# Two buffers for the fill weights of attention and mLSTM, and the mLSTM chunks overlapped in program order, in a hybrid decoder block on one Trainium2 core

## The reference, cut to what matters

```python
# mLSTM: 4 heads of 64, chunks of 128 tokens (8 chunks), carry (C, n, m) from chunk to chunk
D = F[..., :, None] - F[..., None, :] + ig[..., None, :]          # causal
m_t = jnp.maximum(F + m0[..., None], jnp.max(D, axis=-1))
Sw = jnp.einsum('bhctd,bhcsd->bhcts', qc, kc) * jnp.exp(D - m_t[..., None])
num = einsum(Sw, vc) + inter[..., None] * einsum(C0, qc)
h = num / jnp.maximum(jnp.abs(den), jnp.exp(-m_t))[..., None]
h = h * lax.rsqrt(jnp.mean(h * h, axis=-1, keepdims=True) + EPS) * hn_g * jax.nn.sigmoid(o)
# sliding-window attention: 8 query heads, 2 key heads, blocks of 128, window 128, sinks
s = jnp.einsum('bnqkgd,bnskd->bkgnqs', qh, kb);  p = jnp.exp(s - m)
out = jnp.einsum('bkgnqs,bnskd->bnqkgd', p / den, vb)
# merge: g_a * (y_a @ w_br_a) + g_b * (y_b @ w_br_b) + g_c * (y_c @ w_br_c), g = sigmoid(h @ w_gate)
```

## Time and profile before

| | |
|---|---|
| median of 3 runs | 2003.87 us (2002.91 to 2469.56) |
| profiled execution, its own time | 1997.14 us |
| its span, first to last instruction | 1995.4 us |
| granted TensorE clock, mean | 0.960 of full speed |
| PE busy | 1839.7 us, 92% of the span |

### The profile page before, as it was taken

How to read it: one execution, slowest core, us unless ns; L and a number is a source line. 1 busy time by engine, 2 the same in 40 slices (tenths; PEclk the granted TensorE clock), 3 DMA queues, 4 the chain that set the end, 5 groups by cost and what they waited for, 6 DMA issues and landing times.

```text
span 1995.4 us, 37944 instructions
## 1 busy us (share of the span) xinstructions
PE 1839.7 (92%) x16145; PEld 1028.8 (52%) x16145; DVE 665.5 (33%) x1569; ACT 437.6 (22%) x999; POOL 230.5 (12%) x352
## 2 busy tenths in 40 slices
PE   6999999998998599999999999996999999999990
PEld 3454455554443255555555554554566565665550
DVE  4385344443343532333223333552211111000114
ACT  4220412221223321122121212111222222221210
POOL 3030000000000102221022214001000000000003
PEclk9999999998899799999999999996999999999995
DMA  9386010001112000101010028231999999999988
GB/s 312 110 281 220 11 32 21 21 21 32 42 42 65 17 24 24 30 14 30 17 30 22 21 108 307 108 127 65 388 393 395 392 393 393 390 388 388 388 319 319
DMA packets 146919, 334.03 MB, mean 167 GB/s; under 512 B 19274, under 2 KB 63224, under 8 KB 146844
## 3 DMA queue, kind: packets, MB, share of 16 engines
q1 hardware_dynamic: 127776, 282.68, 39.1%
q0 software_dynamic: 8240, 25.04, 3.8%
q10 hardware_dynamic: 10828, 25.24, 3.2%
HBM read 299.50 MB, written 37.63 MB: 169 GB/s over the span
## 4 chain that ended last, share of the span: by engine, by line
PE 84%; DMA 7%; DVE 3%; ACT 2%; issue 1%; POOL 1%; SPq 1%; ACTq 0%; POOLq 0%; DVEq 0%
PE bank L280 80%; DMA arena<-in_w_e_in 3%; DMA arena<-in_w_in 3%; PE bank L1189 1%; POOL arena L711 1%; PE bank L878 1%; DMA arena<-y_slots,ints 1%; PE bank L1206 1%; PE bank L1128 0%; PE bank L1208 0%; SPq L452 0%; DMA y_slots<-arena 0%; DVE arena L1748 0%; DVE arena L1826 0%; PE bank L754 0%
## 5 line engine op out<-in xcount | busy, mean ns | idle before, releaser
L280 PE MATMUL bank<-arena 128*32 128x256 f32 (+8 forms) x15294 | 1746.8, 380 | 60.2 <-DMA arena<-in_w_in 12.9
L280 PEld LDWEIGHTS bank<-arena 128*32 128x32 f32 (+4 forms) x15294 | 937.8, 134 | 811.3 <-issue 545.6
L2191 DVE TENSOR_TENSOR arena<-arena,bank 128x128 f32<-128x128 f32 x96 | 21.8, 283 | 369.8 <-ACT arena L1591 369.8
L1578 ACT ACTIVATE arena<-bank,arena 128x96 f32<-128x96 f32 x256 | 85.9, 441 | 11.8 <-PE bank L1189 11.8
L675 POOL DMA_INDIRECT arena<-xnorm,ints x32 | 31.6, 987 | 470.9 <-PE bank L1189 450.7
L2200 DVE TENSOR_TENSOR arena<-bank,arena 128x512 f32<-128x512 f32 x64 | 35.7, 558 | 134.6 <-PE bank L280 134.6
L1984 DVE TENSOR_TENSOR arena<-arena,bank 128x256 f32<-128x256 f32 x40 | 16.8, 421 | 172.8 <-PE bank L280 172.8
L626 POOL TENSOR_TENSOR arena<-arena 64x256 f32<-64x256 f32 x96 | 71.1, 741 | 28.7 <-DVE arena L1970 22.0
L1584 ACT ACTIVATE arena<-bank 128x384 f32<-128x384 f32 x32 | 15.7, 490 | 267.7 <-PE bank L1208 267.7
L1529 ACT ACTIVATE arena<-bank 128x256 f32<-128x256 f32 (+1 forms) x48 | 18.4, 382 | 208.7 <-PE bank L280 208.7
L1591 ACT ACTIVATE arena<-bank 128x128 f32<-128x128 f32 x96 | 19.7, 278 | 164.7 <-PE bank L280 164.7
(11 more groups left out here) (330 smaller groups left out, 1025.5 us busy)
## 6 DMA issues: line engine op xcount, KB each, us to landing
arena<-in_w_e_in SPq DMA_DIRECT2D x64, 2048.0 KB, 21.3
arena<-in_w_e_out SPq DMA_DIRECT2D x32, 2048.0 KB, 21.4
arena<-in_w_ada SPq DMA_DIRECT2D x12, 2048.0 KB, 12.4
arena<-in_w_in SPq DMA_DIRECT2D x32, 512.0 KB, 4.0
y_slots<-arena ACTq DMA_DIRECT2D x32, 288.0 KB, 6.3
y_slots<-arena POOLq DMA_DIRECT2D x21, 384.0 KB, 17.9
arena<-in_x SPq DMA_DIRECT2D x4, 1024.0 KB, 8.4
arena<-in_w_in SPq DMA_DIRECT2D x2, 2048.0 KB, 25.4
```

Of the source, the lines that this page charges most:

```text
L280: return nc.tensor.matmul(o, l, r, start=start, stop=stop)
L1578: ins = A.activation(e_xT[s][:, k, :], PS[k // 4][:, ts(k % 4, CAP)], ACT.Identity, scale=sc2[:, k:k + 1], bias=sh2[:, k:k + 1])
L2191: ins = TT(e_h[:, r, :], e_g[:, r, :], E_GU[r][:, P:2 * P], ALU.mult)
```

## The change

- SP loads the fill weights alternately into two views, `FWS[0]` and `FWS[1]`, with a semaphore each; the load for chunk f is issued when the fill of chunk f-2 is done. Attention and mLSTM form one sequence of 16 loads.
- Attention's score matmuls alternate between the partition halves (the loop over a is the inner one).
- mLSTM on PE: the opening of chunk c+1 (`b_mu`, scores, transposes of the keys: `front`) comes right after chunk c's fill, and the transposes of chunk c's y (`mlstm_turned`) come after fill 0 to 2 of chunk c+1. The first opening comes right after attention's last fill, and the last y of attention is transposed after the first three fill matmuls of mLSTM, in `PS[7]`. The products with the state come after fill 4 instead of fill 2.
- The mLSTM's temporaries move to places that are free earlier. POOL's copies for mLSTM chunk 0 come ahead of its copies for attention chunk 0; ACT copies the keys of chunk 0 ahead of attention and those of chunk c+1 in the middle of chunk c; DVE makes `b_wv` and `b_bd` of chunk 0 ahead of attention (`weighted`), those of chunk c+1 between L1887 and L1888 of chunk c.
- PE's attention loop and the mLSTM loops of all engines are written out in Python.

```diff
 # SP
-            with sp.Fori(1, NT) as c:
-                sp.wait_ge(sem("fill"), 2 * c)
-                columns(FW, 0, c)
...
+            def fill_columns(f):
+                sp.dma_start(FWS[f % 2], w_in[:, :, ds((0, OFF_G)[f // NT] + P * (f % NT), P)]).then_inc(s_fill[f % 2], 16)
...
+            fill_columns(0)
+            fill_columns(1)
...
+            for f in range(2, 2 * NT):
+                sp.wait_ge(sem("fill"), 2 * (f - 1))
+                fill_columns(f)
+                if f >= NT + 2:
+                    first_gate(f - NT - 1)
 # POOL
+            pool.wait_ge(sem("gates_dve"), B_CLEARED)
+            pool.wait_ge(sem("b_silu"), 4)
+            pool.wait_ge(sem("proj_out"), 34)
+            staged(0)
             def attn(c, first=False):
...
+            for c in range(NT):
                 pool.wait_ge(sem("b_exp"), c + 1)
                 G.tensor_tensor(b_e, b_e, U.unsqueeze(1).to_broadcast([P, H, P]), ALU.mult).then_inc(sem("b_masked"), 1)
+                if c < NT - 1:
+                    staged(c + 1)
 # PE
             def attn(c, first=False):
-                pe.wait_ge(sem("mix_staged"), c + 1)
-                for a in range(2):
-                    for i in range(4):
+                pe.wait_ge(sem("mix_staged"), c + 2)
+                for i in range(4):
+                    for a in range(2):
...
+            def front(c):
+                if c == 0:
+                    pe.wait_ge(sem("gates_act"), G_DONE)
+                    pe.wait_ge(sem("mix_done"), NT - 1)
+                    pe.wait_ge(sem("pa_out"), 2 * NT)
+                else:
+                    pe.wait_ge(sem("mix_staged"), NT + c + 1)
                 pe.wait_ge(sem("b_k"), c + 1)
                 pe.wait_ge(sem("b_bd"), c + 1)
                 mm(PS[0], ones[0:32, :], b_bd[0:32]).then_inc(sem("b_mu"), 1)
...
+            def mlstm(c):
+                fill(c, 0, 3)
+                if c:
+                    mlstm_turned(c - 1)
+                else:
+                    attn_turned(NT - 1)
+                fill(c, 3, 5)
+
+                if c:
                     pe.wait_ge(sem("b_state"), c)
                 pe.wait_ge(sem("b_kt"), c + 1)
                 pe.wait_ge(sem("b_arg"), c + 1)
+                pe.wait_ge(sem("b_wv"), c + 1)
+                pe.wait_ge(sem("mix_done"), NT + c)
...
+            for c in range(NT):
+                attn(c, c == 0)
+                if c < NT - 1:
+                    attn_turned(c)
+            front(0)
+            for c in range(NT):
                 mlstm(c)
+                if c < NT - 1:
+                    front(c + 1)
+            mlstm_turned(NT - 1)
 # ACT, mLSTM
+            for c in range(NT):
+                act.wait_ge(sem("b_scores"), c + 1)
...
                 A.activation(b_e, b_e, ACT.Exp, scale=-1.0).then_inc(sem("b_exp"), 1)
+                if c:
+                    mlstm_out(c - 1)
+                else:
+                    attn_out(NT - 1, PS[7])
...
                 A.activation(ga_o[:, 0:512], PS[5], ACT.Copy).then_inc(sem("ga_out"), 1)
+                if c < NT - 1:
+                    keys(c + 1)
                 root(b_ms, c + 1)
 # DVE, mLSTM
+            def weighted(c):
+                dve.wait_ge(sem("mix_staged"), NT + c + 1 if c else 1)
+                TT(b_wv, b_v, bc(g_w[:, ts(c, 4)], 65), ALU.mult).then_inc(sem("b_wv"), 1)
...
                 lk(TT(b_h, b_h, PS[4][:, 0:260].rearrange("p (h n) -> p h n", h=H), ALU.add))
+                if c < NT - 1:
+                    weighted(c + 1)
                 lk(STT(b_d, b_h[:, :, 64], -1.0, b_h[:, :, 64], ALU.mult, ALU.max))
```

More of the change, by code:

```diff
@@ L925, in mlstm, with mlstm_turned @@
                 ins.then_inc(sem("b_scores"), 1)
-                fill(c, first, 0, 3)
-                if not first:
+            def mlstm_turned(c):
+                pe.wait_ge(sem("mix_y"), NT + c + 1)
+                for p in range(2):
+                    ins = E.transpose(PS[7][:, ts(2 + p, P)], b_hh[:, 2 * p:2 * p + 2, :].rearrange("p a n -> p (a n)"), ident)
+                ins.then_inc(sem("mix_yT"), 1)
+            def mlstm(c):
[6 more added lines that the diff above has]
+                if c:
                     pe.wait_ge(sem("b_state"), c)
@@ L939, in mlstm @@
                 ins.then_inc(sem("b_inter"), 1)
-                fill(c, first, 3, 8)
+                fill(c, 5, 8)
                 pe.wait_ge(sem("b_sw"), c + 1)
@@ L944, in mlstm @@
                 ins.then_inc(sem("b_num"), 1)
[L945 to L951, removed]
+                fill(c, 8, 16)
+            for c in range(NT):
[4 more added lines that the diff above has]
+            for c in range(NT):
                 mlstm(c)
+                if c < NT - 1:
+                    front(c + 1)
+            mlstm_turned(NT - 1)
             pe.wait_ge(sem("mix_done"), NT + NT)
@@ L1438, in attn, with attn_out, keys @@
                 A.activation(c_pT[:, 4:8, :], PS[3], ACT.Copy).then_inc(sem("c_pT_out_a"), 1)
+                if not last:
+                    attn_out(c, PS[0])
+            def attn_out(c, bank):
                 act.wait_ge(sem("mix_yT"), c + 1)
-                A.activation(QC[:, :, ts(c, P)], PS[0].rearrange("p (i n) -> p i n", i=4), ACT.Copy).then_inc(sem("mix_done"), 1)
-            with act.Fori(0, NT) as c:
+                A.activation(QC[:, :, ts(c, P)], bank.rearrange("p (i n) -> p i n", i=4), ACT.Copy).then_inc(sem("mix_done"), 1)
+            def keys(c):
+                if c:
+                    act.wait_ge(sem("b_scores"), c)
+                A.activation(b_k, QK[:, 2:4, ts(c, P)], ACT.Copy, scale=N ** -0.5).then_inc(sem("b_k"), 1)
+            act.wait_ge(sem("b_silu"), 4)
+            keys(0)
+            with act.Fori(0, NT - 1) as c:
                 attn(c)
+            attn(NT - 1, True)
             def root(v, n):
@@ L1898, in mlstm @@
                 TT(b_hh, b_hh, VO[:, ds(c, 1), 256:512].rearrange("p o (h n) -> p (o h) n", h=H), ALU.mult).then_inc(sem("mix_y"), 1)
-            with dve.Fori(0, NT) as c:
+            for c in range(NT):
                 mlstm(c)
-            chain[0] += 11 * NT
             dve.wait_ge(sem("mix_done"), NT + NT)
```

127 lines of the change are left out of this document (52 added, 75 removed).

## The result

The changed kernel takes 1949.46 us (median of 4 runs, 1948.21 to 1950.37), the kernel before on the same chip 2003.39 (4 runs). The ratio is 0.9757, with a 95% interval of 0.9737 to 0.9778: 2.4% faster. It is taken from the fast runs alone, while the median of 2003.39 still counts one slow run of 2469.56, so the quotient of the two medians differs from it. The profiled execution took 1950.37 us, its span is 1948.6 us against 1995.4, so 46.8 us have to be found.

What follows compares the result with a forecast made beforehand. PE's waits and slow clock were taken as the bound. Savings of 11.1 (attention), 5.0 (transition) and 27.9 (mLSTM), 44.0 us, took 1997.14 to 1953.1; adding 6.7 for the median gave 1959.9 us, range 1950 to 1976.

Steps and rivals of the forecast that it cites:

- The median: Whole kernel: the median of runs lies 6.7 us above the profiled execution, raising 1953.1 to 1959.9 us.
- Attention, seams: Attention between chunks: load wait gone and scores alternating, seam 1.93 instead of 3.65 us, 12.0 us saved over 7 seams.
- The rival that the order does nothing: Attention's scores: alternating the halves gains nothing, 7.7 us lost, total 1967.6 us; chance 0.08.
- What is late next: Attention's exponentials and mLSTM's copy of y still come in time for PE, with margins of 0.4 and about 1 us.
- rival 2: Attention's exponentials or mLSTM's copy of y become new waits, 1 us in 15 chunks, total 1974.9 us; chance 0.14.
- The beginning: Attention's start: PE waits for four POOL copies, partly repaid by the new score order; cost 0.8 to 0.9 us.
- Transition: Attention to mLSTM: the first opening waits only for DVE's L1841, not for freed temporaries; 5.0 us saved.
- mLSTM: mLSTM stage: both seam waits and the clock stretch go, eight chunks at 18.43 us, 147.6 against 175.50, 27.9 us saved.
- rival 1: PE's clock still dips at mLSTM seams and attention's start because of weak work, total 1975.1 us; chance 0.17.
- rival 4: Written-out bodies, 16 on PE, must be fetched and stall; at 5.3 us a body 2% slower, 2044 us; chance 0.04.

Runs made afterwards that it cites:

- e_order: The kernel before with only attention's score matmuls alternating between the partition halves: 2006.31 us, ratio 1.0049.
- e_buffers_order: The kernel before with both two fill-weight views and attention's alternating scores: 1972.21 us, ratio 0.9866.
- e_turn_first: The changed kernel with each mLSTM chunk's y transposed at its old place, ahead of the next chunk's opening: 1949.17 us, ratio 0.9765.
- e_copies_first: The changed kernel with POOL's copies for attention chunk 0 again ahead of those for mLSTM chunk 0: 1949.36 us, ratio 0.9746.
- e_buffers: The kernel before with only the two fill-weight views, PE's and SP's chunk loops written out: 1979.20 us, ratio 0.9917.
- the two last ones: e_copies_first, 1949.36 us, and that kernel with attention's fill halves in two banks, y turned in PS[7] and DVE's token shift later, 1940.22 us.
- e_keys_late: The changed kernel with ACT's copy of the next chunk's keys at the end of the chunk, not its middle: 1961.96 us, ratio 0.9836.

## Why the prediction was right, and where its terms were off

The sign, the size and its split over three stages were right. 1949.46 lies half a microsecond below the range's lower end at 1950, and the sum was 44.0 against 46.8 us.

**The median.** Only 2.8 of the 10.4 us between forecast and result lie in the sum. The forecast added 6.7 us, by which the first median (2003.87) stood above the profiled run. The changed kernel's median is 0.9 below its profiled run, which makes the other 7.6. The kernel before's medians beside the later runs, 1994.9 to 1997.1, show that 2003.87, the middle of three runs, was a high one. From 1997 the same sum would have given 1953.

**Attention, seams.** 7 seams at 1.72 were forecast, 12.0 us; a chunk takes 22.67 us as forecast and the stage is 12.5 shorter. By the traces, counted from the first score to the next fill, the seven seams gave 12.6, since the waits for the load differ (0.65 to 1.04). The lower clock at the start took 1.5 back, the new order of chunk 0 gave 1.0, and 0.4 is the last turn of y, which moved. But the two parts of a seam are no separate terms. The order alone brought 1.4 us (e_order), the views alone 5.7, and both 13.4 (e_buffers_order). The sum had the right total because the change makes both. The rival that the order does nothing fell: the scores take 2.00 us, as in the earlier trace rows. Where the prediction weighed the Trainium skill, "TensorE: Matmul & The Clock Gate", Part 3 (matmuls in strict program order), the old order was to take about 3.3 us by the rule (the prediction's estimate). The kernels here with the old order show 2.96 and those with the new one 2.00, and the sum rightly went by the row.

**What is late next.** The margins held. In the changed kernel the exponentials' last step ends 0.4 us before PE's transposes start (348.92 and 349.36), and ACT's copy of y 1.1 before the state products, 0.4 and 1 by the forecast. (The sum in the text, 373.16 + 3.30 + 0.19, is 376.65 and not 376.5. The last two steps overlap by 0.1 us, so the margin stands.) Neither attention's exponentials nor mLSTM's copy of y is among PE's waits (rival 2).

**The beginning.** PE was forecast to wait for four copies, and waits 2.51 us instead of 0.78. The cost in the sum was 0.9. It was more like 1.7 + 1.5 less 0.96, 2.3 us, because the clock fell to 0.50 there in this execution. e_turn_first, the same up to mLSTM but without that dip, shows 1.7 less 0.96, as forecast. e_copies_first took both away, and the total did not follow.

**Transition.** 5.0 forecast, 4.4 to 4.9 measured, depending on whether attention's last turn of y, which moved behind the boundary, is counted.

**mLSTM.** 27.9 forecast, 30.3 measured. The idle term was right (15.2 against 15.1). The rest is a mis-sized term: a chunk takes 18.09 and not 18.43 us, 2.7 us in eight. The 18.43 was the busy time of a chunk with two idle times in it, and the ends of matmuls are modelled. A last record ahead of an idle time is counted whole, though its tail would lie under the next one. "No idle, full clock" is best read from a stretch that has neither.

**The clock, rival 1.** The result was as forecast, full clock, but the argument against the rival was not sound. It rested on chunk 5, whose seam kept a full clock with 2.36 us of idle time. e_order has the same mLSTM instructions, 2.6 us earlier, and all its seams dip, with 24.3 us of stretch. That the timing decides is the reading left by the two traces; it was not tried by itself. The start of attention bears it out: the same instructions after the same 2.5 us of idle time ran at 0.50 in the changed kernel and at 1.00 in e_turn_first. So the full clock was forecast rightly, but not for a reason that held. What the runs support is only that in all four kernels without idle time in mLSTM the clock stayed full there. e_buffers still dips with 1.1 us of idle time at a seam. No kernel with idle time in mLSTM kept it throughout. Part 4 of the Trainium skill's "TensorE: Matmul & The Clock Gate" says that transposes do not count as busy for the clock in the same way. Transposes and products on 32 and 64 rows at every seam did not tip it by themselves in the changed kernel, in e_turn_first or in the two last ones. So taking away the last idle time was worth more than its own length: e_keys_late loses 10.9 us for 7.3 of waiting.

**The unrolled bodies, rival 4.** No stall: 145.09 of 145.10 us busy with all bodies written out.

**What the prediction did not see** is that the second view and the early keys each need the other, and for more than attention. The keys' early copy with one view saves no idle time in mLSTM (16.6 us against 15.1), the view without it leaves 1.1 us a seam, and the place of y's turn decides nothing.

## What to carry to other kernels

When a seam has two waits in a row on one engine, the gain of removing one is what the other doesn't take back; price them together, by the time at which the last of them ends. When an edit moves a load in a DMA queue's list, follow every other transfer in that list to whoever waits for it: a save moved one chunk later cost some 30 us here, against the 47 that the change brings. If short waits recur at a TensorE stage with a granted clock below 1.00, removing them can bring back the clock too: here some 12 us beside the 15.1 of waiting. A removal that leaves one wait in each chunk may keep most of the dips, as e_buffers did.

## What the runs showed of the hardware that was not expected

- Idle times of 1.0 to 2.4 us in each chunk of 18 to 24 us go with dips of the clock in some chunks and not in others: mLSTM's mean was 0.98 in e_keys_late, 0.93 in e_buffers, 0.91 before. Which chunks dip seems to go with the timing, which was not tried by itself. With mLSTM's instructions and idle time unchanged (15.1 and 15.3 us), the time above them was 15.2 us in one kernel and 24.3 in another. The executions of the kernel before alone range from 1992.3 to 2002.0 in one set, with mean clocks of 0.962 to 0.954. One profiled execution therefore doesn't price a clock term to better than some 10 us here.
- The dips move. The changed kernel has none in mLSTM and gained one in the preparation, where 16 records went from 4.77 to 6.51 us.
- Score matmuls on 64 partitions take 0.185 us a record when the heads of one half follow each other, and 0.125 when the halves alternate (2.96 and 2.00 for 16).
